# Latent attention in a fused diffusion step: the order of projections, reciprocals and maxima in the pipeline of heads

## The reference

```python
q = (cq @ w_uq).reshape(B, L, N_HEADS_B, QK_DIM)          # 8 heads, 64 + 32 rotary
q = concatenate([q[..., :NOPE_DIM], apply_axial_rope(q[..., NOPE_DIM:], cos, sin)], -1)
kv = (keys_c @ w_ukv).reshape(B, Lk, N_HEADS_B, NOPE_DIM + V_DIM)   # Lk = 128 + 1024
s = einsum('bqhd,bkhd->bhqk', qi, k) * ATTN_SCALE
p = softmax(s, axis=-1)
o = einsum('bhqk,bkhd->bqhd', p, v)
y = concatenate([y_a * silu(g_a), o * silu(g_b)], -1) @ w_out
```

## Time and profile before

| | us |
|---|---|
| three runs, lowest, median, highest | 1500.98, 1501.81, 1511.92 |
| the profiled execution's own time | 1502.52 |
| its span, first to last instruction | 1500.4 |
| PE busy with matmuls | 1395.9 |
| DVE, ACT, POOL busy | 690.5, 413.0, 217.0 |
| mean granted TensorE clock | 0.961 |

### The profile page before, as it was taken

One profiled execution on the slowest core, in us unless ns is written; L12 is line 12 of the kernel. 1 busy time (PEld: TensorE's weight loads), 2 busy tenths in 40 slices (PEclk: granted clock), 3 DMA queues, 4 the chain that ended last, 5 costly groups with the idle time before them and its releaser, 6 DMA issues.

```text
span 1500.4 us, 17818 instructions
## 1 busy us (share of the span) xinstructions
PE 1395.9 (93%) x6912; PEld 1085.7 (72%) x6912; DVE 690.5 (46%) x938; ACT 413.0 (28%) x737; POOL 217.0 (14%) x163
## 2 busy tenths in 40 slices
PE   6698999999999988898888988999999999999997
PEld 2697999999943456654454544688889999998786
DVE  5611414232334697667876666654422222223643
ACT  2622211121212122243333332445431111112321
POOL 2310000000023000054434434500000000000000
PEclk9798999999989999999999998999999999999999
DMA  8401333333330021300000000122310001003411
GB/s 366 130 2 33 115 120 138 125 113 120 135 115 11 28 92 65 132 6 6 18 9 0 21 0 16 64 72 95 114 33 30 30 30 30 30 30 108 173 43 56
DMA packets 29918, 107.01 MB, mean 71 GB/s; under 512 B 3659, under 2 KB 7951, under 8 KB 26416
## 3 DMA queue, kind: packets, MB, share of 16 engines
q1 hardware_dynamic: 28144, 99.30, 18.6%
q10 hardware_dynamic: 1728, 7.08, 1.2%
HBM read 89.67 MB, written 16.66 MB: 71 GB/s over the span
## 4 chain that ended last, share of the span: by engine, by line
PE 77%; DVE 11%; issue 4%; DMA 3%; POOL 2%; ACT 1%; SPq 0%; DVEq 0%; PEld 0%; POOLq 0%; ACTq 0%; PEldq 0%
PE bank L538 41%; PE bank L972 13%; PE bank L860 5%; PE bank L888 3%; PE bank L846 3%; PE bank L761 2%; PE bank L1039 2%; DMA SCR<-x_sample_in 2%; DVE SCR L1658 1%; POOL fw L1917 1%; PE bank L825 1%; DVE amax_part L1686 1%; DVE SCR L1716 1%; PE bank L697 1%; PE bank L549 1%
## 5 line engine op out<-in xcount | busy, mean ns | idle before, releaser
L538 PE MATMUL bank<-H_r,WR_r 128*128 128x384 f32 x1728 | 352.8, 336 | 1.4 <-DVE H_r L1811 1.2
L538 PEld LDWEIGHTS bank<-H_r,WR_r 128*128 128x128 f32 x1728 | 302.6, 188 | 6.2 <-issue 4.2
L538 PE MATMUL bank<-H_r,SCR_r 128*128 128x384 f32 x480 | 161.5, 337 | 0.0
L1917 POOL TENSOR_TENSOR fw<-fw,SCR 128x1024 f32<-128x1024 f32 x56 | 133.1, 2377 | 124.3 <-ACT SCR L1322 123.3
L1322 ACT ACTIVATE SCR<-bank 128x512 f32<-128x512 f32 x144 | 83.7, 597 | 160.0 <-PE bank L860 140.3
L1881 POOL TENSOR_SCALAR ssq<-ssq 128x1 f32<-128x1 f32 (+1 forms) x36 | 16.1, 446 | 619.3 <-ACT bank L1067 520.3
L538 PE MATMUL bank<-H_r,WX_r 128*128 128x384 f32 x384 | 100.8, 344 | 3.3 <-PEq L637 3.3
L972 PE MATMUL bank<-H_r,WR_r 128*128 128x512 f32 x432 | 99.9, 394 | 3.8 <-DVE SCR L1844 3.8
L972 PEld LDWEIGHTS bank<-H_r,WR_r 128*128 128x128 f32 x432 | 82.2, 190 | 21.3 <-DVE SCR L1844 4.0
L1482 DVE SCALAR_TENSOR_TENSOR SCR<-bank,col,SCR 128x766 f32<-128x766 f32 (+1 forms) x96 | 43.0, 510 | 108.8 <-ACT SCR L1207 107.3
L538 PEld LDWEIGHTS bank<-H_r,SCR_r 128*128 128x128 f32 x480 | 91.0, 190 | 0.0
(11 more groups left out here) (281 smaller groups left out, 2160.1 us busy)
## 6 DMA issues: line engine op xcount, KB each, us to landing
WR<-w_mod_in SPq DMA_DIRECT2D x16, 1024.0 KB, 7.0
SCR<-w_in_in SPq DMA_DIRECT2D x20, 512.0 KB, 3.4
H<-w_mod_in SPq DMA_DIRECT2D x4, 2048.0 KB, 14.3
SCR<-x_sample_in SPq DMA_DIRECT2D x16, 512.0 KB, 15.3
WR<-w_io_in SPq DMA_DIRECT2D x16, 512.0 KB, 3.4
sp_rows<-SCR SPq DMA_DIRECT2D x9, 512.0 KB, 2.6
KV<-sp_rows SPq DMA_DIRECT2D x9, 512.0 KB, 7.6
H<-w_oe_in SPq DMA_DIRECT2D x2, 2048.0 KB, 13.0
```

The costliest lines, as they stand in the source:

```text
L538: last = nc.tensor.matmul(out, l, r, start=(n == 0), stop=(n == len(pairs) - 1))
L1917: ptt(p_acc, pT[0] if kt == 1 else p_acc, pT[kt % 3], ALU.add).then_inc(p_added, 1)
```

## The change

Six edits, all in the attention.

1. `STEPS` becomes q0, kA, kB, q1, q2: PE projects the first third of the queries ahead of the keys, before `row_sums`; kA and kB follow, then `scores(1)`, then q1 and q2. Key banks and waits follow (q1 waits until DVE has read q0 from bank 3, q2 until two key quarters are read). ACT and DVE take q0 first as well, and ACT's `query_his` come one key tile earlier.
2. The reciprocal of the row sums is cut in four of 128 columns: two among the key quarters, two after t = 0 and t = 1.
3. The two halves of the normalised output come after t = 2 and t = 3, and the product with the gate is cut in two halves, after t = 5 and t = 6.
4. In `shifted_scores` the term with the maximum's row comes last, and only it waits for `mx_in`.
5. Before the first head: projections start one convolution result earlier (`CA - 1`), the rotary rows of the second key buffer are split after the maxima instead of before the keys, and the maxima of the first head alternate between banks 3 to 5 and 0 to 2 (`alone`).
6. Fillers: 2 instead of 3 after each of these tiles, 10 instead of 12 after them.

```diff
-STEPS = ("kA", "kB", "q0", "q1", "q2")
+STEPS = ("q0", "kA", "kB", "q1", "q2")
...
-            pe.wait_ge(i_done, CA)
+            pe.wait_ge(i_done, CA - 1)
...
+                b, was = (0, 2 * (t - 2)) if alone and t % 2 else (3, 2 * (t - 1 - alone))
+                if was >= 0:
+                    pe.wait_ge(mx_red, at(i, s, MAXES, was + 1))
...
-                for n, (l, r) in enumerate(((k_hi[m][0:QK + 1, keys], q[0:QK + 1]), (k_hi[m][0:QK, keys], q_lo[m][0:QK, queries]), (k_lo[m][0:QK, keys], q[0:QK]))):
+                for n, (l, r) in enumerate(((k_hi[m][0:QK, keys], q_lo[m][0:QK, queries]), (k_lo[m][0:QK, keys], q[0:QK]), (k_hi[m][0:QK + 1, keys], q[0:QK + 1]))):
+                    if n == 2 and max_row_in is not None:
+                        pe.wait_ge(mx_in, max_row_in)
...
                 if after:
-                    project(i, n, "kA")
+                    project(i, n, "q0")
                 if before:
                     row_sums(i, s - 1)
                 if after:
-                    project(i, n, "kB")
+                    project(i, n, "kA", "kB")
                 scores(i, s, 1)
                 if after:
-                    project(i, n, "q0", "q1", "q2")
+                    project(i, n, "q1", "q2")
...
                     if after:
                         if kt == 0:
+                            query_rows(i, n, 0)
                             keys(i, n, 0, 1, 2, 3)
                         if kt == 1:
-                            query_rows(i, n, 0, 1, 2)
-                        if 2 <= kt <= 4:
-                            query_his(i, n, kt - 2)
+                            query_rows(i, n, 1, 2)
+                        if 1 <= kt <= 3:
+                            query_his(i, n, kt - 1)
...
-                    if before and t in (1, 3, 6):
-                        finish(i, s - 2, (t + 1) // 3)
+                    if before:
+                        if t < 2:
+                            reciprocals(i, s - 2, 2 + t)
+                        elif t < 4:
+                            normalise_output(i, s - 2, t - 2)
+                        elif 5 <= t < 7:
+                            gate_output(i, s - 2, t - 5)
...
+            def reciprocals(i, s, *parts):
+
+                dve.wait_ge(sum_mm, at(i, s, 1, 1))
+                for n in parts:
+                    last = nc.vector.reciprocal(rinv[:, P * n:P * (n + 1)], bank[:, 2, P * n:P * (n + 1)])
+                if parts[-1] == 3:
+                    link(last)
...
                 if after:
-                    key_los(i, n, 0, 1, 2, 3)
-                    queries(i, n, 0, 1, 2)
+                    queries(i, n, 0)
+                    key_los(i, n, 0, 1)
+                    if before:
+                        reciprocals(i, s - 1, 0)
+                    key_los(i, n, 2, 3)
+                    if before:
+                        reciprocals(i, s - 1, 1)
+                    queries(i, n, 1, 2)
                     maxima(i, n, before)
...
+            rope_key_los(0)
+            queries(0, 0, 0)
             key_los(0, 0, 0, 1, 2, 3)
-            queries(0, 0, 0, 1, 2)
-            maxima(0, 0, False)
+            queries(0, 0, 1, 2)
+            maxima(0, 0, False, True)
+            rope_key_los(1)
```

More of the change, by code:

```diff
@@ L827, in project, with max_scores @@
                     last.then_inc(pj_mm, 1)
-            def max_scores(i, s, t):
+            def max_scores(i, s, t, alone=False):
                 m = s % 2
@@ L843, in max_scores @@
                 for n in range(3):
-                    if t and n == 2:
-                        pe.wait_ge(mx_red, at(i, s, MAXES, 2 * t))
-                    last = nc.tensor.matmul(bank[:, 3 + n, 0:KS3], q, k_hi[m][0:QK, KS3 * n:KS3 * (n + 1)], start=True, stop=True)
+                    if was >= 0 and n == 2:
+                        pe.wait_ge(mx_red, at(i, s, MAXES, was + 2))
+                    last = nc.tensor.matmul(bank[:, b + n, 0:KS3], q, k_hi[m][0:QK, KS3 * n:KS3 * (n + 1)], start=True, stop=True)
                     if n:
@@ L1285, in _ @@
             act.wait_ge(i_mm, CA)
-            for m in range(2):
-                nc.scalar.copy(k_hi[m][64:P, :], kT[m][64:P, :]).then_inc(kr_cp, 1)
+            nc.scalar.copy(k_hi[0][64:P, :], kT[0][64:P, :]).then_inc(kr_cp, 1)
             def keys(i, s, *parts):
                 for n in parts:
-                    act.wait_ge(pj_mm, at(i, s, 5, 1 + n // 2))
+                    act.wait_ge(pj_mm, at(i, s, 5, 2 + n // 2))
                     nc.scalar.copy(k_hi[s % 2][0:NOPE, KS4 * n:KS4 * (n + 1)], key_bank(n)).then_inc(pk_his, 1)
@@ L1637, in _, with rope_key_los @@
             dve.wait_ge(i_done, CA)
-            for m in range(2):
+            def rope_key_los(m):
                 dve.wait_ge(kr_cp, m + 2)
@@ L1709, in finish_prompt, with head_rows, out_half, normalise_output @@
                 tt_(y, y, sgate[r, LS:TOK], ALU.mult)
-            def finish(i, s, part):
-                r, c = slice(s % 2 * VD, (s % 2 + 1) * VD), ds1(i + (s // 2 + CA))
-                if part == 0:
-                    dve.wait_ge(sum_mm, at(i, s, 1, 1))
-                    link(nc.vector.reciprocal(rinv, bank[:, 2, :]))
-                if part == 1:
-                    for half in range(2):
-                        h = slice(VD * half, VD * (half + 1))
-                        last = tt_(yT[r, c, 512 * half:512 * (half + 1)].rearrange("p a n -> p (a n)"), bank[h, 6 + s % 2, :], rinv[h, :], ALU.mult)
-                    last.then_inc(o_cp, 1)
-                if part == 2:
-                    dve.wait_ge(o_cp, at(i, s, 3, 2))
-                    y = yT[r, c, 0:LS].rearrange("p a n -> p (a n)")
-                    tt_(y, y, sgate[r, 0:LS], ALU.mult).then_inc(o_cp, 1)
+            def reciprocals(i, s, *parts):
[4 more added lines that the diff above has]
+                    link(last)
+            def head_rows(s):
+                return slice(s % 2 * VD, (s % 2 + 1) * VD)
+            def out_half(i, s, half):
+                return yT[head_rows(s), ds1(i + (s // 2 + CA)), 512 * half:512 * (half + 1)].rearrange("p a n -> p (a n)")
+            def normalise_output(i, s, half):
+                h = slice(VD * half, VD * (half + 1))
+                last = tt_(out_half(i, s, half), bank[h, 6 + s % 2, :], rinv[h, :], ALU.mult)
+                if half:
+                    last.then_inc(o_cp, 1)
+            def gate_output(i, s, half):
+                dve.wait_ge(o_cp, at(i, s, 3, 2))
+                y = out_half(i, s, half)
+                last = tt_(y, y, sgate[head_rows(s), 512 * half:512 * (half + 1)], ALU.mult)
+                if half:
+                    last.then_inc(o_cp, 1)
+            def finish(i, s):
+                reciprocals(i, s, 0, 1, 2, 3)
+                for half in range(2):
+                    normalise_output(i, s, half)
+                for half in range(2):
+                    gate_output(i, s, half)
             def attend(i, s, before=True, after=True):
@@ L1750, in _ @@
             finish_prompt(HEADS // 2 - 1, 1)
-            for part in range(3):
-                finish(HEADS // 2 - 1, 1, part)
+            finish(HEADS // 2 - 1, 1)
             def wo_split_lo(l, h, ks):
```

40 lines of the change are left out of this document (21 added, 19 removed).

## The result

Four runs of the changed kernel have a median of 1481.36 us (1477.02 to 1485.98), four runs of the kernel before on the same chip 1504.69: ratio 0.985, 95% interval [0.982, 0.989]. So it is faster by some 1.5 to 1.7%, where 1482 was forecast. Several terms of the sum were off, though, and their errors cancelled by luck; the experiments are about that.

A forecast was written before the change was run, and what follows sets the result against it. DVE's queue paces the second half of a head, the slow clock adds, PE paces the rest. Start -2.6, reciprocal -8.7 and clock -8.0 sum to -19.3 us: 1502.5 to 1483.2, or 1482 as median; range 1474 to 1506.

The forecast's parts named there:

- Bound and main term: Loop heads: DVE's queue paces the second half, slow clock adds; reciprocal in four pieces saves 8.7 us in six heads.
- 1.44 of the sum: Loop heads: DVE time saved per head, as two of four reciprocal pieces hide among the key quarters.
- The clock: Loop heads: half-rate stretch behind PE's idle goes, 1.5 us a head plus 3.0 in the sixth; 8.0 us counted.
- the third that was held back: Loop heads: doubtful third of the 12 us clock gain, not counted because remaining idle of 1.45 us might slow the clock.
- the clock falls anyway: Rival, loop heads: remaining PE idle still lowers the clock, leaving only reciprocal's 8.7 and start's 2.6 us: 1491; chance 0.22.
- The query third: Third projected ahead of keys: last rotation stays chained to POOL's second addition; value 0, ends -1.0 and +0.3 us a head.
- the rival in which the third brings 1476: Query third ahead removes PE's 0.97 us idle before the maxima in all six heads: 1476 us; chance 0.06.
- in the first head itself, without reciprocal and gate, 0: First head, which has no reciprocal or gate: the change was to alter its time by 0 us.
- Output and gate in halves: Loop heads: same work; value 0 if gate's first half precedes POOL's sixth addition, ends -0.3 and +1.5 us a head.
- Its rival: POOL's sixth addition starts before the gate's first half, PE idles 2.9 us and the clock falls: 1506; chance 0.22.
- The start: Before the first head: -2.6 us, from dropped L1640 1.4, two bank sets 0.8 and max row 0.4.
- After the last head: DVE needs 0.4 us more for the finish, covered by 1.0 us of fillers: 0; last head bound by POOL's additions.

The follow-up runs named there:

- the pieces alone: Kernel before with only the row sums' reciprocal cut in four 128x128 pieces; normalisation, gate, query third, first head and max row as before: 1478.74 us, ratio 0.984.
- the keys first: Changed kernel with both key passes ahead of the three query thirds again on every engine, all else kept: 1471.42 us, ratio 0.980.
- the delayed gate: Changed kernel with a small unused 64x32 VectorE reciprocal ahead of the gate's first half in every loop head: 1504.26 us, ratio 0.999.
- the same delay: Changed kernel with keys ahead of queries, values copied after the third tile's maxima in loop heads, and the small reciprocal ahead of the gate: 1471.45 us, ratio 0.980.
- the one with the earlier copy: Changed kernel with keys ahead of queries and, in loop heads, values copied after the third tile's maxima instead of the sixth's: 1471.87 us, ratio 0.979.

## Why the forecast held, and where its steps did not

*Bound and main term: right.* DVE's queue set the pace and the slow clock added to it. Undoing the pieces returned the 2.89 us, the fall and all of the 23 us; the pieces alone gave all of them. In the loop the kernel before and the pieces alone differ in nothing else, so their rows show how the two terms part. From the first maxima of a head to the fourth it takes 6.79 us (725.96 to 732.75) for 8.39 (725.39 to 733.78), at the full clock in both: 1.60 for the 1.44 of the sum. From there to the context tile, where the slow stretch lay, it takes 12.26 (745.01) for 14.23 (748.01, below): 1.97 for the 1.5 of the sum.

*The clock: right in kind, too small.* I counted two thirds of 12 us. No loop head of the changed kernel fell (one of six did with the pieces alone), so the third that was held back, 4.0 us, was wrong, and "the clock falls anyway" (1491) with it. The size was off as well: a head became 3.3 to 3.6 us shorter for 1.44 + 1.5 worked out (the sixth 6.5, for 3.0 more). The 4.0 held back and the 0.6 us in each of six heads, less what the query third costs, come to about 6 of the 7.1 us by which the loop gained more than the forecast; the rest is open.

Two readings behind the third that I held back were wrong. I left PE an idle time of 1.45 us; it is 0.42 and 0.49 in the changed kernel (ahead of 684.88 and 687.29), since PE has other matmuls to do during part of the wait at each of the two places, and I had taken that off once only. And I judged the clock by two rows, 1.47 us without a fall and 1.60 with one. The head that I read has an idle time of 1.60 us of its own in the same place, and behind it the clock stayed at 1.00; one of 1.38 us in the pieces alone was followed by a fall. From the kernel before, timeline and window:

```profile
748.01 0.33 PE L841 MATMUL bank<-WR_r 96*128 96x128 f32 x1 [1.60 <-DVE amax_part L1686]
```

```profile
748.01:753.58 5.57, 5.57 (x28) 2.77 (x28) 1.66 (x4) 1.69 (x4) 3.06 (x2) 1.00 0.42 142
```

So between 1.38 and 1.60 us these runs show both outcomes. The longest idle time of a loop head in the changed kernel is 0.91 us, clear of them.

*The query third: the step that failed.* "Value 0" held for the wait itself: L1667 still stands beside the second addition, and the rival in which the third brings 1476 fell. But it costs 0.27 us a head, at my upper end of 0.3, and the sentence "in the first head itself, without reciprocal and gate, 0" was wrong by 5.3 us. There, at 635.10, the last rotation does get in front of the second addition, POOL's later additions shift, and the sixth comes 1.0 us earlier (650.08 for 651.07 with the keys first): it came 0.66 us behind the copy of the values there, and comes 0.43 us ahead of it here. My text had this case, with the third addition directly behind the second, but followed it no further than that third addition. I had listed what waits for POOL as operations with two SBUF inputs; the copy has one and waits all the same. The Trainium skill ("SBUF — State Buffer", Who interferes with whom) says so: a copy can go through both port pairs and then contends with GpSimd for the shared one. The trace agrees: the copy took 2.28 us beside the addition and 0.47 ahead of it.

*Output and gate in halves: right, by 0.14 us.* I could not tell the two starts apart; the trace has the gate ahead by 0.13 to 0.19 us in all six heads (0.12 to 0.22 when it was run again). The work is not quite the same, as I had it: the second half waits (1.31 to 1.51 us), but PE idles for only 0.48 us at most behind it. Its rival was priced well: 24 us above the forecast, 26 measured. The rule that I had cited from the Trainium skill (same page and section), that whoever starts first holds the lock and the other is blocked whole, agrees with the delayed gate that waited (2.86 us), with the same delay that cost nothing once the lead was larger, and with the addition stretched to 2.76 us. But who started first is not to be read to a tenth of a microsecond in the trace: an addition shown 0.11 us ahead gave way (695.12), and one shown 0.03 us ahead did not (736.16).

*The start: right in kind, too small.* -4.75 us for -2.6 in the profiled executions. Most of it comes ahead of the first maxima, where I stayed at the lower end: they start 9.0 us after the convolution's end (606.28 - 597.31) for 11.8, 2.8 sooner for 1.4. That PE's earlier projections bring what the dropped L1640 doesn't is argued; they were not undone by themselves. The two bank sets take 0.9 us out of the maxima (14.5 for 15.4, from the first to the transpose), 0.8 forecast; the max row 0.6, 0.4 forecast. When the edits to the first head are undone together, the first scores come 3.3 to 3.6 us later in the traces, and the medians are 2.3 to 2.6 longer.

*After the last head: right*, the cover of the fillers held.

So the mechanism held and the total was luck in part: a first head that lost 5.3 us met a loop that won 7.1 more. The versions with the keys first, 1471.4 to 1471.9, beat both kernels; the one with the earlier copy has the wider lead. The keys first without the halves, where the gate has no such race, was not run.

## What to carry to other kernels

A long instruction on the pacing engine is worth cutting where a piece fits into a time in which that engine waits anyway; what the cut saves on the path may be less than what it saves on TensorE's clock (1.60 and 1.97 us a head here), so look at the longest idle time of PE and what follows it. Look at every such row before judging, not at one of each kind. Before moving a step, list every VectorE instruction that touches the memory GpSimd uses, copies included, with its lead over GpSimd's next start: a lead of 0.14 us is luck, and losing it cost as much as the whole change brought. When several edits come together, undo each by itself: here one of them took back a quarter of what another had won.

## What the runs showed that was not expected

- The wait works both ways: a GpSimd addition of 128x1024 took 2.36 us alone, 2.69 to 2.78 when VectorE's gate half had started 0.12 to 0.22 us before it, and up to 2.96 in the delayed version.
- A copy from SBUF to SBUF with one source waited as long as an operation with two: 2.28 us for 0.47.
- Length alone doesn't decide which idle time of PE the clock falls behind. Those of 1.34 and 1.47 us were not followed by a clock of 0.50, one of 1.38 was; of two of 1.60 one was, at 925.09, and one was not, at 748.01; in the heads those of 2.76, 2.89 and 3.05 all were, and the stretch behind then lasted 6.8 us in most cases, 3.4 to 13.7 in others. Ahead of the first head of the changed kernel PE idled for 3.60 us up to 600.63, and the clock fell only at 605.54, in the next idle time (2.81 us up to 606.28).
